# mLSTM heads in six PSUM banks, second attention with its value tile first, cosine products in PSUM, a reordered first stage, and attention weights brought to rows by transposing

## The chip, the cores and the metric

The kernel runs on one NeuronCore of a Trainium2 chip. A core has five engines with an instruction stream each: TensorE (PE), which multiplies matrices into PSUM, VectorE (DVE), ScalarE (ACT), GpSimd (POOL) and SyncE (SP), which here issues the DMAs of the weights. They meet through semaphores. SBUF holds operands; PSUM has 8 banks of 128 x 512 float32. The metric is the device time of one execution in microseconds.

## What is computed

Two blocks over 512 tokens of 1024 channels, one batch, float32. Cut to what matters:

```python
def first_block(x, ...):                   # mLSTM and pooling
    u = rms_norm(x, norm_in_g[l]); proj = u @ w_in[l]      # 4096 columns
    # pooling branch: window means (2, 4, 8, 16) minus u, a 256x256 map per group, scale, times silu(gate)
    # mLSTM branch: conv of 5 taps, silu, block-diagonal q, k, v, gates, 4 heads of 256
    h_fwd = mlstm_chunkwise(qh, kh, vh, log_i[0], log_f[0])
    h_bwd = flip(mlstm_chunkwise(flip(qh), flip(kh), flip(vh), ...))
    h = h_fwd + h_bwd                      # num / max(|den|, exp(-m)) in each direction
    h = (h - mu) * rsqrt(var + EPS)        # per token and head
    out = h * mh_norm_w + skip_w * c       # then times silu(gate)
    x = x + concat(pool, mlstm) @ w_out[l]
def second_block(x, ...):
    # i = 0: NSA attention (compressed, selected, window branch; 16 heads of 64, 4 key groups)
    # i = 1: sliding-window attention (SWA): 16 heads, 2 key groups, biases, a sink in the softmax denominator
    x = x + mixer(rms_norm(x, norm_mix[i]))
    x = x + (silu(causal_conv(a)) * u) @ w_down           # gated FFN of 2816 channels
    return rms_norm(x, norm_final)
def apply_rope(x, cos, sin): ...          # x*cos + swapped(x)*sin, on queries and keys
```

## The kernel before

**Tiles.** Activations lie channel-major, as 8 tiles of 128 channels x 512 tokens. Every projection is a list of weight tiles of 128 x 1024: `in` 32, `wo_pool` 8, `wo_m` 8, `nsa` 21, `nsa_o` 8, `gu0` 44, `down0` 22, `swa` 10, `swa_o` 8, `gu1` 44, `down1` 22, in all 227. SP loads them in turn into 4 buffers (`raw`); the load of tile w waits for `tile_split` of tile w-4. ACT rounds a tile to its high part (`high(w)`, the cast of L424), POOL subtracts that from it for the low part (L390, signal `tile_split`), both into 2 buffers. PE multiplies high by high, high by low and low by high for each of 8 channel tiles k: 24 matmuls of 128 x 512 (L1470 to L1472, `channel_major`) into one bank, signal `tile_used`. DVE or ACT takes the bank (`freed`). The activations are split the same way (`xh_ready`, `xl_ready`).

**Order.** Every engine's program is written out by hand; no scheduler is at work. `RING` and `BANK` say which PSUM bank a tile of a stage goes to.

**The start.** ACT casts weight tile 0, makes eight x_hi (L442), casts tile 1, squares the eight x tiles for the norm (`square`, L434; each from the fourth on waits for an addition of DVE, L817), issues the DMAs of 13 constants from its own queue (`constants`, L415), casts tile 2. DVE makes eight x_lo (L809). The 32 `in` tiles come in the order conv (8), pooling (8), pooling gate (8), mLSTM gate (8).

**From `in` to the heads.** PE merges k and v maps, computes k1 (banks 2 and 3 in turn, `k_out`), transposes values (`vt_mm`, DVE copies `vt_out`), and computes gates. DVE first makes the eight low parts for `wo_pool` (L837, line 952 is the copy of the values that PE waits for) and then the value copies.

**The heads.** For head h: `wo_pool` tiles of `POOL_TILES`, `maxima_rows(h+1)`, `head_scores(h+1)` into banks 2 to 5, then `numerators(h)`: for each of 4 token tiles i and 2 directions a sum of matmuls 128 x 257 (L1611) into bank n % 2:

```python
n = 8 * h + 2 * i + d
if n >= 2:
    pe.wait_ge((fwd_out, bwd_out)[d], NT * h + i)
```

So PE waits at each token tile until ACT (`forward_out`, L508) and DVE (`head_out`, L1020) have emptied the bank of the tile before. ACT's exponentials of the decay (L531) go into 2 buffers `WE`. After the last head ACT and DVE normalise H (`xhat`, `xhat_last` L1061), PE transposes it, DVE adds the skip term (`add_skip`, L1052), POOL multiplies by the gate (L396), and ACT copies each result as the high part of `wo_m`'s input (L554), for which `wo_m`'s first tile waits at L1447.

**NSA.** `rotary` (L1099 on, in `nsa` and in `swa`) is four DVE operations: sine product (L1104) and cosine product (L1105) into SBUF, a shuffle (L1111), a sum (L1115). In `nsa` the two products read PSUM. Attention goes through 48 units (token tile, heads in one or two pairs, branch): `score`, DVE's row maxima, ACT's exponentials, `turn` (PE transposes, L1743), ACT and DVE copies (L686), `output` (L1764). The softmax weights of a unit, one number per token and head, are spread over the channels by matmuls of an identity with a broadcast column (L1756).

**SWA.** `norm(4)` runs after tile 1 of the projection. Tile j: DVE multiplies by 1/rms into an SBUF buffer `TB` (L1392), ACT adds the bias there (`add_bias`, L768), DVE turns it (`rotary`, all operands in SBUF). Tile 0 is the key, 1 to 8 the queries, 9 the values, which PE transposes (L1514) once the last has its bias. Then come 16 units of two pairs.

## Time and profile before

| quantity | value |
|---|---|
| median of 3 runs | 1728.25 us (1727.33 to 1728.44) |
| the profiled execution's own time | 1723.56 us |
| its span in the trace | 1721.6 us |
| mean granted TensorE clock | 0.985 |
| PE busy | 1637.9 us, 95% |
| first SWA weight tile, first matmul | 1154.50 us |
| NSA attention units | 590 to 749.89 us |

The page gives the busy time of each engine; the trace gives every instruction with start, length, the idle time before it and what ended that. Matmuls of a row overlap, so lengths add up to more than the time between starts. A clock of 1.00 is 2.4 GHz, 0.5 is 1.2 GHz.

### The profile page before, as it was taken

To read this page: it belongs to the slowest core of one execution; us is meant where nothing else is said; L and a number is where in the kernel's file an instruction comes from. 1 tells how busy PE (TensorE), PEld (TensorE's weight loads), DVE (VectorE), ACT (ScalarE), POOL (GpSimd) and SP (SyncE) were. 2 spreads that over 40 slices of the span, in tenths; PEclk is the share of its full clock that TensorE was granted. 3 is DMA by queue.
4 is the path that set the end of the run, shared out by engine and by line. 5 is a ranking of instruction groups with operands and counts; after the bars stand their busy time and mean duration, and the time that the engine had idled before them with its cause. 6 is when DMAs were issued, how large, how long until landed. Compare 5 with 4: busy or idle time off the path is not lost.

```text
span 1721.6 us, 21467 instructions
## 1 busy us (share of the span) xinstructions
PE 1637.9 (95%) x8324; PEld 1280.4 (74%) x8324; DVE 1011.3 (59%) x1390; ACT 632.4 (37%) x1228; POOL 648.2 (38%) x421
## 2 busy tenths in 40 slices
PE   6999998979999999999999999999799999999996
PEld 4888655657788766678888888887567888888884
DVE  5995244575884466645655555448662755556444
ACT  4222333253562566634222222233462422223223
POOL 2444301134442133234444444434234444444442
PEclk9999999989999999999999999999899999999998
DMA  6222201005221100013322223222101322222221
GB/s 233 98 91 96 82 13 37 25 25 189 86 98 62 38 2 2 2 38 98 98 94 94 96 97 110 98 86 91 45 2 62 98 98 96 95 94 97 97 98 49
DMA packets 37670, 133.83 MB, mean 78 GB/s; under 512 B 4609, under 2 KB 5057, under 8 KB 37057
## 3 DMA queue, kind: packets, MB, share of 16 engines
q1 hardware_dynamic: 34992, 123.22, 21.4%
q10 hardware_dynamic: 2576, 9.24, 1.5%
q8 instruction: 66, 1.08, 0.3%
q14 instruction: 36, 0.29, 0.1%
HBM read 130.35 MB, written 2.10 MB: 77 GB/s over the span
## 4 chain that ended last, share of the span: by engine, by line
PE 84%; DVE 8%; ACT 3%; issue 3%; POOL 1%; ACTq 0%; DMA 0%; DVEq 0%; POOLq 0%
PE ps L1470 17%; PE ps L1471 17%; PE ps L1472 17%; PE ps L1806 4%; PE ps L1804 4%; PE ps L1805 4%; PE ps L1728 3%; PE ps L1743 3%; PE ps L1764 2%; PE ps L1523 2%; PE ps L1756 1%; DVE sb_arena L1115 1%; PE ps L1611 1%; DVE sb_x_lo L809 1%; ACT sb_arena L674 1%
## 5 line engine op out<-in xcount | busy, mean ns | idle before, releaser
L390 POOL TENSOR_TENSOR sb_w_lo<-sb_raw,sb_w_hi 128x1024 fp32r<-128x1024 f32 x227 | 556.1, 2450 | 858.1 <-ACT sb_w_hi L424 829.8
L1470 PE MATMUL ps<-sb_x_hi,sb_w_hi 128*128 128x512 f32 x1384 | 545.2, 394 | 23.4 <-ACT sb_x_hi L442 10.6
L1471 PE MATMUL ps<-sb_x_lo,sb_w_hi 128*128 128x512 f32 x1384 | 541.5, 391 | 0.0
L1472 PE MATMUL ps<-sb_x_hi,sb_w_lo 128*128 128x512 f32 x1384 | 541.3, 391 | 0.0
L424 ACT CAST sb_w_hi<-sb_raw 128x1024 fp32r<-128x1024 f32 x227 | 238.6, 1051 | 622.4 <-PE ps L1472 448.3
L1470 PEld LDWEIGHTS ps<-sb_x_hi,sb_w_hi 128*128 128x128 f32 x1384 | 261.5, 189 | 83.9 <-POOL sb_w_lo L390 17.1
L1472 PEld LDWEIGHTS ps<-sb_x_hi,sb_w_lo 128*128 128x128 f32 x1384 | 261.6, 189 | 55.3
L1471 PEld LDWEIGHTS ps<-sb_x_lo,sb_w_hi 128*128 128x128 f32 x1384 | 261.7, 189 | 54.2 <-issue 0.7
L1329 DVE TENSOR_TENSOR sb_x_lo<-sb_arena,sb_x_hi 128x512 fp32r<-128x512 f32 x44 | 98.4, 2243 | 104.4 <-ACT sb_x_hi L728 104.4
L1806 PE MATMUL ps<-sb_x_hi,sb_w_lo 128*128 128x512 f32 x336 | 130.7, 389 | 0.0
L1804 PE MATMUL ps<-sb_x_hi,sb_w_hi 128*128 128x512 f32 x336 | 130.7, 389 | 0.0
L1805 PE MATMUL ps<-sb_x_lo,sb_w_hi 128*128 128x512 f32 x336 | 130.7, 389 | 0.0
L1337 DVE TENSOR_TENSOR sb_arena<-ps,sb_rstd 128x512 f32<-128x512 f32 x44 | 30.4, 691 | 154.7 <-PE ps L1472 154.6
L1341 DVE SCALAR_TENSOR_TENSOR sb_arena<-sb_arena,sb_cols 128x512 f32<-128x512 f32 x44 | 115.8, 2632 | 1.6
L674 ACT ACTIVATE sb_arena<-ps,sb_small 128x256 f32<-128x256 f32 (+3 forms) x192 | 93.6, 497 | 55.9 <-DVE sb_small L1252 55.9
L723 ACT ACTIVATE sb_arena<-sb_arena 128x512 f32<-128x512 f32 x44 | 27.8, 633 | 150.5 <-DVE sb_arena L1343 150.4
L1252 DVE TENSOR_REDUCE sb_small<-ps 128x2 f32<-128x768 f32 (+3 forms) x48 | 50.3, 1048 | 53.0 <-PE ps L1732 53.0
L1728 PE MATMUL ps<-sb_arena 64*128 64x256 f32 (+3 forms) x384 | 74.5, 466 | 1.6 <-ACT sb_arena L781 0.9
L1806 PEld LDWEIGHTS ps<-sb_x_hi,sb_w_lo 128*128 128x128 f32 x336 | 63.1, 188 | 13.2
L1805 PEld LDWEIGHTS ps<-sb_x_lo,sb_w_hi 128*128 128x128 f32 x336 | 63.1, 188 | 13.2
L1804 PEld LDWEIGHTS ps<-sb_x_hi,sb_w_hi 128*128 128x128 f32 x336 | 63.1, 188 | 12.9
L1743 PE MATMUL ps<-sb_ident,sb_arena 128*128 128x128 f32 x432 | 59.7, 278 | 8.6 <-ACT sb_arena L686 6.3
(257 smaller groups left out, 1889.0 us busy)
## 6 DMA issues: line engine op xcount, KB each, us to landing
sb_raw<-in_w SPq DMA_DIRECT2D x227, 512.0 KB, 3.3
sb_resid<-in_x SPq DMA_DIRECT2D x8, 256.0 KB, 6.0
sb_arena<-in_cmp_w1k ACTq DMA_DIRECT2D x1, 2048.0 KB, 10.5
sb_arena<-in_cmp_w1v ACTq DMA_DIRECT2D x1, 2048.0 KB, 14.5
out<-sb_resid SPq DMA_DIRECT2D x8, 256.0 KB, 2.1
sb_arena<-in_pool_w ACTq DMA_DIRECT2D x1, 1024.0 KB, 5.0
sb_arena<-in_invc ACTq DMA_DIRECT2D x1, 1024.0 KB, 7.0
sb_arena<-in_wg ACTq DMA_DIRECT2D x1, 768.0 KB, 8.4
```

What stands on the lines that cost most here:

```text
L390: nc.gpsimd.tensor_tensor(WL[:, w % SPL], raw[:, w % RAW], WH[:, w % SPL].bitcast(F32), ALU.subtract).then_inc(tile_split, 1)
L424: nc.scalar.copy(WH[:, w % SPL], raw[:, w % RAW]).then_inc(hi_made, 1)
L674: ins = nc.scalar.activation(PE_[:, v % 2, hh, n * r:n * (r + 1)], PS[:, 2 + 2 * (v % 2) + hh, n * r:n * (r + 1)], ACT.Exp, bias=nmr[:, v ...
L1341: step.mark(nc.vector.scalar_tensor_tensor(CV[:, b], AP_[:, b, 1:1 + S], w[1], CV[:, b], ALU.mult, ALU.add))
L1470: mm(out, WH[:, s, k], XH[:, k], start=(k == 0), stop=False)
L1471: mm(out, WH[:, s, k], XL[:, k], start=False, stop=False)
L1472: ins = mm(out, WL[:, s, k], XH[:, k], start=False, stop=(k == KT - 1))
L1728: mm(s_[hh], QN[half, c + r, P * i:P * (i + 1)], K[half, k0:k0 + n], start=True, stop=False)
L1743: ins = nc.tensor.transpose(PS[:, 6 + hh, P * n:P * (n + 1)], PE_[:, v % 2, hh, P * n:P * (n + 1)], ident[:])
L1804: mm(psum(k), WH[:, s, k], XH[:, x], start=False, stop=False)
L1805: mm(psum(k), WH[:, s, k], XL[:, x], start=False, stop=False)
L1806: ins = mm(psum(k), WL[:, s, k], XH[:, x], start=False, stop=(f == FT - 1))
```

## The change

1. **Start.** DVE splits weight tile 0 in place of ACT and POOL; x tiles come from SP's and ACT's queues in turn; the first gain's columns are a DMA of their own; the 13 constants are issued by SP, behind the loads of weight tiles 0 to 3 and ahead of tile 4's. PE takes tile 0 in the order high x high, low x high, high x low (`first_tile`), tile 1 with its low part last. The `in` tiles are interleaved (`IN_ORDER`).
2. **After `in`.** Value copies and low parts alternate on DVE; a copy of k1 waits for its own tile of `xl_ready`, no longer for all eight; the first score tile goes ahead of the gate placement.
3. **Heads.** Numerators take banks 2*(i%3)+d; `WE` has 8 buffers; ACT and DVE interleave head h+1's decay with head h's output; both directions' denominators are one DVE operation; one `wo_pool` tile per head; the last one and the transposes of the finished heads lie around the last head's numerators; `wo_m`'s first high parts don't wait for the whole of `wo_pool`.
4. **Rotation.** The cosine product is written back into the PSUM bank that it reads.
5. **Both attentions.** DVE writes the weight of a unit spread over 64 channels (`WN`), and PE transposes that.
6. **SWA.** The value tile comes first; `norm(4)` after tile 2; scaling, bias and rotation happen in the tile's own PSUM bank; the last query tile lies between scores and the first turn; queries 8 and 9 are turned inside the attention; the projection starts when one `down0` tile is added, not eight; unit order changed.

```diff
+IN_ORDER = [t for n in range(8) for t in (2 * n, 2 * n + 1, 16 + n)] + list(range(24, 32))
+SWA_ORDER = [9, *range(9)]
-RING = {"in": [0, 1, 2, 3, 4, 5, 6], ..., "swa": [0, 1, 2, 3, 4, 5]}
+RING = {"in": [0, 1, 2, 3, 4, 5, 6], ..., "swa": [4, 5, 2, 3, 0, 1, 4, 6, 0, 1]}
...
+            dve.wait_ge(raw_in[0], 16)
+            nc.vector.tensor_copy(WH[:, 0], raw[:, 0]).then_inc(w0_hi, 1)
+            dve.wait_ge(w0_hi, 1)
+            nc.vector.tensor_tensor(WL[:, 0], raw[:, 0], WH[:, 0].bitcast(F32), ALU.subtract).then_inc(w0_lo, 1)
...
-            for k in range(KT):
-                lo("wo_pool", k, SZ[:, k])
-
             nc.vector.memset(V1[:, :, :, 256:257], 1.0)
             for j in range(KT):
                 dve.wait_ge(vt_mm, j + 1)
...
+                lo("wo_pool", j, SZ[:, j])
...
             def numerators(h):
                 pe.wait_ge(p_ready, 8 * (h + 1))
                 for i in range(NT):
+                    if i == NT - 1:
+                        pe.wait_ge(fwd_out, NT * h + 1)
+                        pe.wait_ge(bwd_out, NT * h + 1)
                     for d in range(2):
-                        n = 8 * h + 2 * i + d
-                        if n >= 2:
-                            pe.wait_ge((fwd_out, bwd_out)[d], NT * h + i)
...
-                            ins = mm(PS[:, n % 2, 0:257], PW[d][:, at:at + P], V1[:, j, h], ...)
+                            ins = mm(PS[:, 2 * (i % 3) + d, 0:257], PW[d][:, at:at + P], V1[:, j, h], ...)
...
+            for h in range(HEADS - 1):
+                maxima_rows(h + 1)
+                numerators(h)
+                head_scores(h + 1)
+                pe.wait_ge(fwd_out, NT * (h + 1))
+                pe.wait_ge(bwd_out, NT * (h + 1))
+                channel_major("wo_pool", 4 + h, KT)
...
+            turn_head(0)
+            turn_head(1)
+            numerators(HEADS - 1)
+            for j in range(2, 6):
+                turn_head(j)
...
+            channel_major("wo_pool", KT - 1, KT)
+            for j in range(6, KT):
+                turn_head(j)
             linear("wo_m")
...
-            def rotary(src, c_, s_, out, scale, signal, first=None):
...
+            def rotary(src, c_, s_, out, scale, done):
+
+                dve.wait_ge(freed, done - 1)
                 step.mark(nc.vector.scalar_tensor_tensor(TS, src, -scale, s_, ALU.mult, ALU.mult))
-                ins = nc.vector.scalar_tensor_tensor(TM, src, scale, c_, ALU.mult, ALU.mult)
...
+                step.mark(nc.vector.scalar_tensor_tensor(src, src, scale, c_, ALU.mult, ALU.mult))
                 step.mark(nc.vector.stream_shuffle(TS, TS, swap))
                 step.wait()
...
-                nc.vector.tensor_tensor(out, TM, TS, ALU.add).then_inc(rope_in, 1)
+                nc.vector.tensor_tensor(out, src, TS, ALU.add).then_inc(freed, 1)
...
-                        for hh in range(2):
-                            mm(PS[DH * hh:DH * hh + DH, v % 2, P * (2 + r):P * (3 + r)],
-                                     wn[:, v % 4, hh, r:r + 1].broadcast_to([P, DH]), ident[:], start=True, stop=True)
+                        nc.tensor.transpose(PS[:, v % 2, P * (2 + r):P * (3 + r)], WN[:, v % 2, r], ident[:])
...
-            pe.wait_ge(down_added, KT)
-            linear("swa", 10, 4)
-            turn_values(10, TB[:, 1], qb_ready, 10, 5)
-            pe.wait_ge(tok_out, 5)
-            pe.wait_ge(rope_in, 14 + 9)
-            attention(SWA_UNITS, len(NSA_UNITS), True)
+            pe.wait_ge(down_added, 1)
+            linear("swa", 9, 4)
+            attention(SWA_UNITS, len(NSA_UNITS), True, None, lambda: channel_major("swa", 9, 10))
```

The order of the instructions at three places. ACT at the start, from the cast of weight tile 1 on (`raw_in1` is its DMA, `sq_acc` DVE's additions), before:

```order
L424 CAST sb_w_hi<-sb_raw 128x1024 [waits raw_in1]
L434 ACTIVATE sb_arena<-sb_resid 128x512 x3
L434 ACTIVATE sb_arena<-sb_resid 128x512 [waits sq_acc] x5
L415 DMA sb_arena<-in_wqkv 128x96 [waits zero_set]
L415 DMA sb_arena<-in_bdm 128x32
L415 DMA sb_arena<-in_pool_w 128x2048
L415 DMA sb_arena<-in_invc 128x2048
```

and now:

```order
L452 CAST sb_w_hi<-sb_raw 128x1024 [waits raw_in1]
L462 ACTIVATE sb_arena<-sb_resid 128x512
L462 ACTIVATE sb_arena<-sb_resid 128x512 [waits sq_acc] x5
L452 CAST sb_w_hi<-sb_raw 128x1024 [waits tile_used,raw_in2]
L474 ACT_TABLE_LOAD
L474 ACTIVATE sb_small<-sb_small 128x1
L476 ACTIVATE sb_arena<-ps,sb_small 128x512 [waits sq_sum]
```

The cast of tile 2 stands directly behind the squares; 13 DMA instructions stood there. PE at the numerators of the first head (128x257), before, one bank per direction:

```order
L1611 MATMUL ps<-sb_arena 128x257 [waits p_ready,freed]
L1611 MATMUL ps<-sb_arena 128x257 x4
L1611 MATMUL ps<-sb_arena 128x257 [waits fwd_out]
L1611 MATMUL ps<-sb_arena 128x257
L1611 MATMUL ps<-sb_arena 128x257 [waits bwd_out]
L1611 MATMUL ps<-sb_arena 128x257 x2
```

and now (L1739 is the next head's maxima, L1670 its scores):

```order
L1739 MATMUL ps<-sb_arena,sb_ident 128x512
L1754 MATMUL ps<-sb_arena 128x257 [waits freed,p_ready]
L1754 MATMUL ps<-sb_arena 128x257 [waits freed]
L1754 MATMUL ps<-sb_arena 128x257 x13
L1754 MATMUL ps<-sb_arena 128x257 [waits bwd_out,fwd_out]
L1754 MATMUL ps<-sb_arena 128x257 x4
L1670 MATMUL ps<-sb_arena 128x512 [waits bwd_out,fwd_out]
```

Fifteen numerator matmuls stand ahead of the first wait for an emptied numerator bank. DVE in the SWA projection, before:

```order
L1392 TENSOR_TENSOR sb_arena<-ps,sb_rstd 128x512 [waits tile_used]
L1104 SCALAR_TENSOR_TENSOR sb_arena<-sb_arena 128x512 [waits rope_in,qb_ready]
L1105 SCALAR_TENSOR_TENSOR sb_arena<-sb_arena 128x512
L1111 STREAM_SHUFFLE sb_arena<-sb_arena 128x512 [waits dve_step]
L1115 TENSOR_TENSOR sb_arena<-sb_arena 128x512 [waits dve_step]
```

and now:

```order
L1488 TENSOR_TENSOR ps<-ps,sb_rstd 128x512 [waits tile_used] x2
L1194 SCALAR_TENSOR_TENSOR sb_arena<-ps,sb_arena 128x512 [waits freed,qb_ready]
L1196 SCALAR_TENSOR_TENSOR ps<-ps,sb_arena 128x512 [waits dve_step]
L1197 STREAM_SHUFFLE sb_arena<-sb_arena 128x512
L1199 TENSOR_TENSOR sb_arena<-ps,sb_arena 128x512 [waits dve_step]
```

All but the shuffle have an operand in PSUM now.

## Rows read from the trace of the kernel before

**Rows 1.** The page: the span, and part 1, busy time of each engine.

```profile
span 1721.6 us, 21467 instructions
...
PE 1637.9 (95%) x8324; PEld 1280.4 (74%) x8324; DVE 1011.3 (59%) x1390; ACT 632.4 (37%) x1228; POOL 648.2 (38%) x421
```

**Rows 2.** The windows view: us, busy PE, PEld, DVE, ACT, POOL, clock, DMA share, GB/s.

```profile
0.00:40.00 40.00, 23.73 (x76) 18.47 (x77) 22.68 (x27) 17.21 (x25) 10.47 (x11) 0.91 0.70 251
...
199.00:244.00 45.00, 40.80 (x163) 20.02 (x162) 18.78 (x29) 20.84 (x32) 2.37 (x1) 1.00 0.06 21
...
258.00:378.00 120.00, 103.95 (x399) 71.41 (x396) 63.10 (x202) 46.48 (x102) 17.12 (x9) 0.97 0.10 31
378.00:432.00 54.00, 48.98 (x196) 37.16 (x194) 33.83 (x35) 20.44 (x29) 29.18 (x14) 0.91 0.43 158
...
580.00:750.00 170.00, 164.07 (x1569) 109.92 (x1568) 107.91 (x247) 106.25 (x363) 50.87 (x111) 1.00 0.01 5
...
1154.00:1214.00 60.00, 56.16 (x241) 44.70 (x242) 52.85 (x61) 23.21 (x31) 24.12 (x10) 1.00 0.25 83
1214.00:1221.00 7.00, 0.53 (x3) 0.10 (x1) 6.71 (x9) 1.67 (x3) 2.50 (x2) 0.81 0.26 82
1221.00:1298.00 77.00, 68.84 (x596) 44.55 (x596) 44.85 (x117) 44.68 (x179) 21.07 (x59) 0.91 0.02 8
```

**Rows 3.** Who PE waited for, whole span: us in total, times, longest.

```profile
PE ps L1447 <- ACT sb_x_hi L554: 4.6, 7, 1.0
PE ps L1560 <- DVE sb_arena L952: 2.5, 1, 2.5
```

**Rows 4.** Timeline of the start: start, length, engine, line, operands, [idle before <-releaser].

```profile
10.65 0.77 PE L1470 MATMUL ps<-sb_x_hi,sb_w_hi 128*128 128x512 f32 x1 [10.65 <-ACT sb_x_hi L442]
...
27.67 1.04 ACT L424 CAST sb_w_hi<-sb_raw 128x1024 fp32r<-128x1024 f32 x1 [5.96 <-issue]
...
39.85 1.05 ACT L424 CAST sb_w_hi<-sb_raw 128x1024 fp32r<-128x1024 f32 x1 [8.11 <-PE ps L1472]
45.29 1.05 ACT L424 CAST sb_w_hi<-sb_raw 128x1024 fp32r<-128x1024 f32 x1 [4.38 <-PE ps L1472]
...
31.19 0.80 PE L1470 MATMUL ps<-sb_x_hi,sb_w_hi 128*128 128x512 f32 x1 [5.62 <-POOL sb_w_lo L390]
...
8.26 9.01 DVE L809 SCALAR_TENSOR_TENSOR sb_x_lo<-sb_resid,sb_cols,sb_x_hi 128x512 fp32r<-128x512 f32 x8 [8.26 <-ACT sb_x_hi L442]
17.18 5.46 DVE L817 TENSOR_TENSOR sb_arena<-sb_arena 128x512 f32<-128x512 f32 x7
```

**Rows 5.** PE in the heads: the group of the numerators, and one wait.

```profile
L1611 PE MATMUL ps<-sb_arena 128*128 128x257 f32 x160 | 40.2, 401 | 6.9 <-ACT sb_arena L508 5.0 <-DVE sb_arena L1020 1.1 <-DVE sb_resid L846 0.8
...
294.27 1.13 PE L1598 MATMUL ps<-sb_arena,sb_ident 32*128 32x512 f32 x4 [2.29 <-ACT sb_arena L531]
```

**Rows 6.** Timeline of POOL ahead of the second output projection.

```profile
377.75 11.39 POOL L396 TENSOR_TENSOR sb_arena<-sb_arena 128x512 f32<-128x512 f32 x7 [1.85 <-DVE sb_arena L1052]
```

**Rows 7.** PE in both attentions: the weight matmuls of the first, a piece of a unit of the second.

```profile
L1756 PE MATMUL ps<-sb_ident,sb_small 128*64 128x128 f32 x256 | 24.5, 291 | 0.3 <-DVE sb_arena L1295 0.3
...
1258.34 0.66 PE L1756 MATMUL ps<-sb_ident,sb_small 128*64 128x128 f32 x8
1258.83 1.03 PE L1764 MATMUL ps<-sb_arena 128*64 128x256 f32 x8
...
1261.95 1.06 PE L1743 MATMUL ps<-sb_ident,sb_arena 128*128 128x128 f32 x8 [0.17 <-ACT sb_arena L686]
```

**Rows 8.** DVE's rotation: one group of the first stage, then POOL and DVE in the second.

```profile
L1105 DVE SCALAR_TENSOR_TENSOR sb_arena<-ps,sb_arena 128x512 f32<-128x512 f32 x14 | 9.5, 681 | 0.0
...
1200.74 2.39 POOL L390 TENSOR_TENSOR sb_w_lo<-sb_raw,sb_w_hi 128x1024 fp32r<-128x1024 f32 x1 [3.12 <-ACT sb_w_hi L424]
...
1200.98 2.71 DVE L1115 TENSOR_TENSOR sb_arena<-sb_arena 128x512 f32<-128x512 f32 x1
```

**Rows 9.** PE at the end of the second attention's projection.

```profile
1221.77 1.12 PE L1514 MATMUL ps<-sb_ident,sb_arena 128*128 128x128 f32 x4 [7.24 <-ACT sb_arena L768]
```

583 lines of the change are left out of this document (355 added, 228 removed).

## The prediction

> **What bounds the kernel now.** I read the page first: TensorE is busy for 1637.9 of 1721.6 us [rows 1], and the weight tiles alone need 24 matmuls each on it. The change takes no weight tile away. So almost all that it can win is time in which PE stands still or runs at its low clock, and it can win that only in the stretches that it touches. The next view is the windows [rows 2], which I cut where PE's waits lie. PE's idle time is a stretch's length less its busy time, and (1 - clock) times the length is what the low clock costs in it, roughly, since only busy time counts:
>
> - 199 to 244: 45 - 40.80 = 4.2 us idle, clock 1.00.
> - 258 to 378, the heads: 120 - 103.95 = 16.1 idle, and 0.03 x 120 = 3.6 of clock.
> - 378 to 432, the second output projection: 54 - 48.98 = 5.0 idle, and 0.09 x 54 = 4.9 of clock.
> - 580 to 750, the NSA attention: 170 - 164.07 = 5.9 idle, clock 1.00.
> - 1154 to 1214, the SWA projection: 3.8 idle. 1214 to 1221: 6.5 idle, almost the whole stretch. 1221 to 1298, its attention: 8.2 idle, and 0.09 x 77 = 6.9 of clock.
>
> Then the waits and the timeline, to see what ends the idle time. For the value copies PE waits once for 2.5 us, and 4.6 us for the high parts of the second output projection [rows 3]. At the start PE stands 5.62 us ahead of 31.19; POOL, named as the releaser, had itself waited for the cast at 27.67, and that for 5.96 us of ACT's own DMA issues [rows 4].
>
> **The change part by part.** The sum is made against the profiled execution, 1723.56 us, which is 4.7 below the median of the runs; the forecast adds 4.7 again.
>
> *The start.* Of the 13 DMAs that ACT issued nothing is left on its queue; on SP's they stand behind tiles 0 to 3, so at worst tile 4 comes later, and its place is two tiles of PE work further on. Now the cast of tile 2 follows the squares, and these follow DVE's additions. The eight low parts took 9.01 us, one addition 5.46 / 7 = 0.78 [rows 4]. POOL's first split now waits for all eight, so I price these at 0.78 too: 6.2 us, from 8.26 to 14.5 (DVE's two new operations on weight tile 0 come before x is there). POOL's split of tile 1 then takes about 2.4, as at 1200.74 [rows 8], and holds one addition; six more end at 14.5 + 2.4 + 4.7 = 21.6, the last square a step before, at about 20.6. The cast (1.04) and the split (2.4) bring tile 2 to 24.1 in place of 31.19, 7.1 us. Tile 2 ran at half clock: ACT's casts, which wait for the ends of tiles, start at 39.85 and 45.29, so a tile takes 5.44, and tile 2 took 39.85 - 31.19 = 8.7. With no long stop ahead of it, 3.2 come back. Together 10.3, of which I take **10**. Bounds: 12 if tile 2 starts as soon as tile 1 ends, 6 if the squares end two or three us later. The new order of the `in` tiles I cost at nothing: PE is the cover, 5.44 us a tile, against conv work on DVE which now has two other tiles beside it. If the cover is gone a tile waits 1 or 2 us.
>
> *After `in`.* The copies of the values no longer stand behind eight low parts: 2.5 [rows 3], and the k1 copies, the exp tables and the early score tile take the rest of 4.2 [rows 2]. I take **4**, bounds 3 and 4.2.
>
> *The heads.* With two banks PE stopped at each token tile; the 160 numerator matmuls (40.2 us) had 6.9 us of idle time before them, and the exponentials in two buffers gave waits such as 2.29 us at 294.27 [rows 5]. With six banks fifteen matmuls go through, and what stands behind them (scores, a `wo_pool` tile of 5.44) covers ACT and DVE. What is recoverable is 16.1 + 5.0 + 3.6 + 4.9 = 29.6. What is late next is the tail behind the last head. Six of eight turned tiles can be skipped, gated and copied ahead; the last two can't. POOL's gate takes 11.39 / 7 = 1.63 each [rows 6], twice that is 3.3, an ACT copy and a DVE addition with their handovers some 1.2, and POOL's split of the next weight tile stands behind it, another 1.5 or so: 6 left. So **23.5**, bounds 15 (half of the idle time moves to other waits, with some clock) and 29.6. What could hold DVE here is told under the first rival.
>
> *Rotation.* In the first attention's projection the cosine product reads PSUM and takes 681 ns [rows 8]; written back to PSUM I price it the same. In SWA all operands were in SBUF, and there DVE's sum took 2.71 us at 1200.98 while POOL's split ran from 1200.74 to 1203.13 [rows 8]; the additions at the start, with POOL idle, took 0.78. DVE was busy for 52.85 of 60 us there [rows 2] and so set the pace. Now each operation but the shuffle has an operand in PSUM. Five operations of about 0.7 make 3.5 a tile against PE's 5.44: DVE catches up, even though `norm(4)` comes one tile later.
>
> *SWA.* Of the 3.8 idle in the projection I take 3. The stop of 7.24 us ahead of 1221.77 [rows 9] was the last tile's scaling, queued on DVE behind rotations, its bias on ACT and then the value transposes; with the value tile first that chain lies beside weight tiles, and the stop's 6.5 shrink to 0.5: 6. The low clock in 1214 to 1298 came with that stop; PE had been at 1.00 before it [rows 2]. Of its 6.9 I give back 5, since short waits remain. Of 8.2 idle in the attention I take 3.5, the turned weights in it. Sum **17.5**, bounds 13 and 22.
>
> *Weights by transposing.* In a unit of two pairs the eight weight records start at 1258.34 and the products with the values at 1258.83: 0.49. Eight transposes of the same size take 1.06 [rows 7], so two about 0.22: 0.27 less a unit of two pairs, and 0.16 less, in the same ratio, one of one pair. The first attention has 16 and 32 of them: 4.3 + 5.1 = 9.4 if PE were all that counts. It is not: units hang on maxima, exponentials and copies too, as the 0.17 for ACT before 1261.95 shows. DVE's wider write of the weights (128 x 128 or 256 in place of a few columns, some 0.2) lies in DVE's idle time, 170 - 107.91 = 62 us [rows 2]; uncovered it would cost up to 48 x 0.2 = 10 and leave no gain. I take **5**, bounds 0 and 8.5.
>
> Sum: 10 + 4 + 23.5 + 5 + 17.5 = 60. 1723.6 - 60 = 1663.6, and 4.7 more is **1668**.
>
> **The rivals.**
>
> *The heads give little (0.20).* DVE's normalisation and low parts there are SBUF operations, POOL's gate and splits run beside them, and DVE's sum shows what that does [rows 8]: 0.7 becomes 2.7. Eight such meetings cost 16 us of DVE time behind the last head. For it: PE's 4.6 us for the copies of ACT, which are downstream of POOL and DVE [rows 3]. Against: most of these operations now have a `wo_pool` tile and transposes in front of them. Gain 10 there in place of 23.5: 1682.
>
> *SWA stays bound by DVE (0.12).* If an operation that writes PSUM is held by POOL as one in SBUF is, or takes over a microsecond, a tile takes 5.5 again, and with the later norm the stop only moves. Gain 7 in place of 17.5: 1679. Against it: the mean of 681 ns over 14 operations [rows 8], in a stage in which POOL splits tiles as well.
>
> *Nearly all goes (0.15).* The upper bounds, 12 + 4.2 + 29.6 + 8 + 21 = 75: 1653. For it: each stop also brings a low clock, so what removes the one gives both.
>
> *Slower: the clock in the attentions (0.02).* Transposes take the place of matmuls in a stretch where they already are a large part. If PE's granted clock fell to 1.2 GHz there, each us of work would cost another. The work is 164.1 and, at full clock, some 62 us [rows 2], 226 in all; it decides when over 60 of that run at the low level, and with all of the first attention the time is 1668 + 164 = 1832. Against it: the clock is 1.00 over 580 to 750 with transposes in each unit [rows 2]. The Trainium skill has a rule that speaks for it, in "TensorE: Matmul & The Clock Gate", section "Part 4: PE-mode transpose": the full clock does not engage for transpose mode, which does not count as busy in the same way. By that rule more transposes could bring the low level; the trace shows none of it with the mixture that there is.
>
> **How the numbers follow.** The likeliest case has 0.48, with its own range 1658 to 1678. The first two rivals together (about 1692) have 0.015, and no gain by several partial failures 0.015, of which 0.01 lies within 0.2%. The range is 1650 to 1690: it holds the likeliest case, the first three rivals nearly whole, and leaves out both tails. About 0.2% (3.5 us) is what a measurement of this kernel can tell from no change. All cases but the last two lie far below that: faster 0.965, same 0.01, slower 0.025.
>
> **What the profile after would show.** Tile 2 starts at 23 to 25.5, and tile 3 at 29 to 31. Between 199 and 244 PE's busy share is over 97%. The numerators have under 2 us of idle time before them, and the first NSA tile comes 38 us or so earlier (10 + 4 + 23.5). DVE's last rotation operation in SWA takes 0.7 beside POOL's split. No stop over 2 us lies between the SWA projection and its attention, and the clock there is 0.97 or more. Units of the first attention are 0.1 shorter. The forecast is wrong if the waits reappear under other names: PE before `wo_m` waiting for ACT or POOL for more than 8 us, PE in SWA waiting for DVE at each tile, or PE in the attentions waiting for `weight` on DVE.

## The result, and the profile after

The changed kernel takes 1664.78 us (1663.86 to 1666.39) against 1727.85 (1727.33 to 1728.44): a ratio of 0.9636, 95% interval 0.9619 to 0.9653. It is 63.1 us faster. The forecast was 1668, range 1650 to 1690. The profiled execution took 1663.86 us, the sum had given 1663.6 for it. The 4.7 us that I added for the distance between the profiled execution and the median of before did not exist after: 0.9 us lie there now.

The page after, part 1, answers to [rows 1]:

```profile
span 1662.1 us, 20890 instructions
...
PE 1616.0 (97%) x8036; PEld 1267.8 (76%) x8036; DVE 994.2 (60%) x1360; ACT 630.1 (38%) x1230; POOL 645.7 (39%) x420
```

The span is 59.5 us shorter and PE busy for only 21.9 us less, so 37.6 us of the gain are idle time. The rest is PE at full clock for longer, with less to do, or with fewer restarts. The windows after (columns as in [rows 2]; PE's busy time is the second number, the clock the third from the right):

```profile
0.00:40.00 40.00, 32.34 (x116) 24.13 (x117) 28.06 (x31) 18.62 (x26) 12.79 (x12) 1.00 0.72 264
190.00:232.00 42.00, 41.00 (x165) 20.35 (x163) 19.05 (x29) 21.75 (x35) 2.37 (x1) 1.00 0.06 22
232.00:343.00 111.00, 110.85 (x467) 82.10 (x465) 64.09 (x168) 49.41 (x108) 24.50 (x13) 1.00 0.10 34
343.00:392.00 49.00, 44.59 (x183) 35.75 (x182) 29.70 (x33) 20.20 (x28) 23.16 (x11) 0.93 0.48 178
540.00:705.00 165.00, 156.83 (x1365) 101.79 (x1364) 115.66 (x246) 104.83 (x362) 50.90 (x111) 1.00 0.01 5
1108.00:1168.00 60.00, 59.68 (x274) 47.47 (x273) 47.47 (x73) 27.80 (x45) 24.80 (x10) 1.00 0.28 97
1168.00:1238.60 70.60, 62.09 (x475) 38.10 (x473) 50.89 (x131) 41.96 (x169) 23.34 (x60) 0.95 0.03 9
```

The 1.00 in the first row hides a low clock: the trace's records of the granted clock begin at 17 us. Before that the spacing of the matmuls shows it: 0.43 us apart up to about 17 us and 0.23 us behind, which are the levels of 1.2 and 2.4 GHz. The same holds for the 0.91 of before in [rows 2].

The heads (third row) have 0.15 us of idle time in 111, where [rows 2] had 16. The SWA projection (sixth) has 0.3, and the stop behind it is gone. What has not gone is in the fourth and the last row: 4.4 us idle and a clock of 0.93 in the second output projection, 8.5 idle and 0.95 in the SWA attention. Who PE waits for now:

```profile
PE ps L1911 <- ACT sb_arena L732: 11.0, 15, 2.2
PE ps L1595 <- ACT sb_x_hi L470: 7.7, 2, 7.5
PE ps L1560 <- ACT sb_x_hi L594: 4.4, 3, 3.0
PE ps L1583 <- DVE sb_arena L1382: 1.8, 2, 1.0
```

The first row is the turn of a unit's exponentials in both attentions, waiting for the copy out of the bank that it writes. The waits for numerators and for the value transposes of [rows 3], [rows 5] and [rows 9] are not in it.

Where the time went, from the first matmuls of weight tiles (and the last one of `in`) in both traces, beside my terms, all in us:

| from, to | before | after | gain | forecast |
|---|---|---|---|---|
| start, last matmul of `in` | 198.95 | 189.87 | 9.1 | 10 |
| to `wo_pool` tile 0 | 45.45 | 41.91 | 3.5 | 4 |
| to `nsa` tile 0 | 188.03 | 160.62 | 27.4 | 23.5 |
| to `nsa_o` tile 0 | 317.46 | 312.52 | 4.9 | 5 |
| to `swa` tile 0 | 404.61 | 403.63 | 1.0 | 0 |
| to `swa_o` tile 0 | 143.61 | 130.04 | 13.6 | 17.5 |
| to the end | 423.5 | 423.5 | 0.0 | 0 |

### The profile page after: what moved, and what is told of

Its sections match the earlier page's. It is cut to its first block, busy times and chain, and to the rows that moved or that the text cites. A ratio compares the mean times of both kernels' runs of the same rounds, so it can differ in the third digit from the quotient of the medians.

```text
span 1662.1 us, 20890 instructions
## 1 busy us (share of the span) xinstructions
PE 1616.0 (97%) x8036; PEld 1267.8 (76%) x8036; DVE 994.2 (60%) x1360; ACT 630.1 (38%) x1230; POOL 645.7 (39%) x420
## 4 chain that ended last, share of the span: by engine, by line
PE 89%; DVE 4%; issue 3%; ACT 2%; POOL 1%; DMA 0%; DVEq 0%; ACTq 0%; SPq 0%; POOLq 0%
PE ps L1583 18%; PE ps L1585 18%; PE ps L1584 18%; PE ps L1976 4%; PE ps L1977 4%; PE ps L1978 4%; PE ps L1896 3%; PE ps L1930 3%; PE ps L1911 3%; PE ps L1670 1%; ACT sb_arena L720 1%; PE ps L1754 1%; PE ps L1570 1%; PE ps L1640 1%; PE ps L1692 1%
## 5 line engine op out<-in xcount | busy, mean ns | idle before, releaser
L1583 PE MATMUL ps<-sb_x_hi,sb_w_hi 128*128 128x512 f32 x1368 | 536.9, 392 | 2.2 <-DVE sb_arena L1382 1.8
L1585 PE MATMUL ps<-sb_x_hi,sb_w_lo 128*128 128x512 f32 x1368 | 532.7, 389 | 0.0
L1584 PE MATMUL ps<-sb_x_lo,sb_w_hi 128*128 128x512 f32 x1368 | 532.5, 389 | 0.0
L1583 PEld LDWEIGHTS ps<-sb_x_hi,sb_w_hi 128*128 128x128 f32 x1368 | 257.1, 188 | 59.1 <-issue 3.0
L1584 PEld LDWEIGHTS ps<-sb_x_lo,sb_w_hi 128*128 128x128 f32 x1368 | 257.0, 188 | 54.3 <-issue 1.4
L1585 PEld LDWEIGHTS ps<-sb_x_hi,sb_w_lo 128*128 128x128 f32 x1368 | 256.9, 188 | 53.6
L1978 PE MATMUL ps<-sb_x_hi,sb_w_lo 128*128 128x512 f32 x336 | 130.7, 389 | 0.0
L1976 PE MATMUL ps<-sb_x_hi,sb_w_hi 128*128 128x512 f32 x336 | 130.7, 389 | 0.0
L1977 PE MATMUL ps<-sb_x_lo,sb_w_hi 128*128 128x512 f32 x336 | 130.7, 389 | 0.0
L1978 PEld LDWEIGHTS ps<-sb_x_hi,sb_w_lo 128*128 128x128 f32 x336 | 63.1, 188 | 13.1
L1976 PEld LDWEIGHTS ps<-sb_x_hi,sb_w_hi 128*128 128x128 f32 x336 | 63.1, 188 | 13.1
L1977 PEld LDWEIGHTS ps<-sb_x_lo,sb_w_hi 128*128 128x128 f32 x336 | 63.1, 188 | 13.0
```

The costliest lines, as they stand in the source:

```text
L1583: mm(out, WH[:, s, k], XH[:, k], start=(k == 0), stop=False)
L1584: mm(out, WH[:, s, k], XL[:, k], start=False, stop=False)
L1585: ins = mm(out, WL[:, s, k], XH[:, k], start=False, stop=(k == KT - 1))
L1976: mm(psum(k), WH[:, s, k], XH[:, x], start=False, stop=False)
L1977: mm(psum(k), WH[:, s, k], XL[:, x], start=False, stop=False)
L1978: ins = mm(psum(k), WL[:, s, k], XH[:, x], start=False, stop=(f == FT - 1))
```

## The experiments

Stage times below are those of this table, each from one profile. Two things limit what they tell.

A stop of 0.81 us ahead of `nsa` tile 0 is in some profiles (before, and runs 1, 2, 5, 8, 11 and 12) and not in others (after, and the rest). Behind it PE takes that tile at the pace at which ACT makes its high parts: pairs of matmuls start 0.54 to 0.62 us apart in place of 0.46, at a granted clock of 1.00. Together this is 2.2 us, 1.0 in the heads' stage and 1.2 in the next. What decides it was not tried. I call it the floating stop below; it makes spans less comparable than stages.

Stages that a run doesn't touch also differ. With the second attention as in the changed kernel its stage takes 129.1 to 130.7 us in eight profiles; the first attention with transposed weights takes 166.7 to 166.9 us, counted from the last `nsa` weight tile, in eleven. The medians of before that stand beside the runs lie between 1725.8 and 1728.7 us, so medians alone don't tell 2 us from nothing.

**1. The weights by matmul again.**

```diff
-                        nc.tensor.transpose(PS[:, v % 2, P * (2 + r):P * (3 + r)], WN[:, v % 2, r], ident[:])
+                        for hh in range(2):
+                            mm(PS[DH * hh:DH * hh + DH, v % 2, P * (2 + r):P * (3 + r)],
+                                     wn[:, v % 4, hh, r:r + 1].broadcast_to([P, DH]), ident[:], start=True, stop=True)
...
```

> The changed kernel with the softmax weights of both attentions spread by matmuls with a broadcast column again, nothing else undone. My account: the 4.9 us by which the first attention is shorter come from here, and part of the second one's too. 256 matmul pairs come back, 16 units x 0.27 and 32 x 0.16 on PE in the first (9.4), 16 x 0.27 in the second (4.3), of which about half shows: the first attention 4 to 6 us longer, the second 1 to 3, the kernel 1670 to 1673. Rival: the units are bound by the chain over maxima, exponentials and copies, and the attention got shorter by the other edits around it; then both stay within 1 us and the kernel at 1665 to 1666.

Measured: 1669.42 us, ratio 0.9658 (0.9643 to 0.9673). From the last `nsa` weight tile to `nsa_o` tile 0 it takes 170.33 us, as before (170.36), against 166.65 after: 3.7 us are the weights. The SWA stage is 0.4 longer (130.45), which lies within what that stage varies by. The rival for the first attention falls; for the second it holds.

**2. The weights alone, in the kernel before.**

```diff
-                        for hh in range(2):
-                            mm(PS[DH * hh:DH * hh + DH, v % 2, P * (2 + r):P * (3 + r)], ...)
+                        nc.tensor.transpose(PS[:, v % 2, P * (2 + r):P * (3 + r)], WN[:, v % 2, r], ident[:])
...
```

> The kernel before with only the softmax weights brought to rows by transposing. My account: it brings here what it brings in the changed kernel, 4 to 6 us in the first attention and 1 to 3 in the second: 1720 to 1723. Rival: in the second attention the clock is low for other reasons and the chain binds, so 4 to 5 in all. A low granted clock in the attentions from the transposes would show as a longer time, which I do not expect.

Measured: 1722.73 us, ratio 0.9976 (0.9965 to 0.9987). The first attention 166.72 against 170.36, so 3.6 us, the SWA stage 142.60 against 143.61, 1.0. The 4.6 in all are the rival's size; the 1.0 in the second attention is less than what its stage varies by. The windows view of the first attention, in the kernel before and in this run, each from its last `nsa` weight tile to its first of `nsa_o`:

```profile
579.53:749.89 170.36, 164.43 (x1571) 110.18 (x1569) 107.80 (x247) 106.25 (x363) 50.78 (x110) 1.00 0.01 5
...
584.31:751.03 166.72, 158.53 (x1378) 103.40 (x1377) 116.82 (x247) 106.26 (x363) 51.11 (x110) 1.00 0.02 5
```

PE is idle for 8.2 us where it was 5.9, and busy for 5.9 us less: that much the transposes took off PE, and 3.6 of it shows. DVE is busy for 9.0 us more, 0.19 for each of the 48 units, which is its wider write. The clock is 1.00 with 64 transposes more in it and 256 matmul records fewer (a float32 matmul leaves two records, a transpose one).

**3. Two banks for the numerators.**

```diff
-                    if i == NT - 1:
-                        pe.wait_ge(fwd_out, NT * h + 1)
-                        pe.wait_ge(bwd_out, NT * h + 1)
                     for d in range(2):
+                        if i >= 1:
+                            pe.wait_ge((fwd_out, bwd_out)[d], NT * h + i)
...
-                            ins = mm(PS[:, 2 * (i % 3) + d, 0:257], ...)
+                            ins = mm(PS[:, d, 0:257], ...)
```

> The changed kernel with the numerators in two banks again, one per direction, PE waiting at each token tile for the banks of the tile before; order and all else as changed. My account: the banks are the larger part of what the heads gained; the waits of before come back, 6.9 us over four heads, with some low clock: 8 to 14 us, 1673 to 1679, seen at the numerators. Rival: the order behind the numerators (scores, a weight tile) and the later statistics on DVE made the gain; then PE waits 1 to 3 us in all and the kernel is at 1666 to 1668.

Measured: 1682.28 us, ratio 0.9737 (0.9720 to 0.9754): 17.5 us slower than the changed kernel, more than either account. The wait, and for comparison the numerators of the changed kernel, which have none (the page's groups: busy, mean | idle ahead):

```profile
PE ps L1753 <- ACT sb_arena L539: 14.4, 12, 1.2
```

```profile
L1754 PE MATMUL ps<-sb_arena 128*128 128x257 f32 x160 | 35.7, 382 | 0.0
```

Twelve waits, three in each of the four heads, 1.15 to 1.23 us each, 14.4 in all; PE's numerators, stopped and restarted, are also busy for 38.9 us in place of 35.7, and with that the heads are 17.6 us longer (126.65 against 109.02). In the kernel before the waits had cost 6.9 us [rows 5].

Why so much more? One thing that changed in the order is that ACT makes the next head's exponentials between its outputs. That is not it: behind the last head ACT has none to make, and its three waits are as long. One of them, in this run:

```profile
336.90 2.40 PE L1753 MATMUL ps<-sb_arena 128*128 128x257 f32 x10
339.35 0.16 DVE L1092 SCALAR_TENSOR_TENSOR sb_dn<-ps,sb_arena 128x2 f32<-128x2 f32 x1 [1.27 <-PE ps L1753]
339.54 0.16 DVE L1094 TENSOR_TENSOR sb_dn<-ps,sb_dn 128x2 f32<-128x2 f32 x1
...
339.74 0.17 DVE L1096 RECIPROCAL sb_dn<-sb_dn 128x2 f32<-128x2 f32 x1
339.94 0.48 ACT L539 ACTIVATE sb_arena<-ps,sb_dn 128x256 f32<-128x256 f32 x1 [2.77 <-DVE sb_dn L1096]
340.46 2.44 PE L1753 MATMUL ps<-sb_arena 128*128 128x257 f32 x10 [1.15 <-ACT sb_arena L539]
```

The stop is a chain with nothing beside it: both directions' numerators end, DVE makes both denominators in three operations, ACT takes the forward bank out, and only then PE may write it again. Before, each direction had denominators of its own, so the forward bank was emptied while PE made the backward numerators, and the three waits of a head for ACT and DVE were 0.26 to 0.41 us in the first three heads (in the last, where ACT also normalised between its outputs, up to 2.29). So with two banks the joint denominators of the change cost more than the old ones; six banks hide them. No run had two banks with separate denominators in the new order, so this cause is read from the trace and not tried.

**4. Two buffers for the exponentials**, made behind the four outputs of a head, with DVE's products of a head in one piece.

```diff
-                    if n >= 8:
-                        act.wait_ge(p_ready, n - 7)
+                    if n >= 2:
+                        act.wait_ge(p_ready, n - 1)
...
                 for i in range(NT):
-                    decay(h + 1, i)
                     forward_out(h, i)
+                for i in range(NT):
+                    decay(h + 1, i)
```

> The changed kernel with two buffers for the decay exponentials in place of eight, and ACT making them behind the four outputs of a head, not between them (DVE's products of a head in one piece then). My account: waits of 1 to 2.3 us per head come back at the next head's scores or products, three or four times, 4 to 8 us: 1669 to 1673. Rival: a weight tile (5.44 us) and the scores stand in front of the next numerators and cover it: within 1 us of 1665.

Measured: 1665.50 us, ratio 0.9639 (0.9624 to 0.9653). `wo_pool` and heads take 109.86 against 109.02 us. The rival holds: scores and a weight tile cover the exponentials, and eight buffers bring under 1 us.

**5. The cosine product in SBUF**, for the second attention alone.

```diff
-                step.mark(nc.vector.scalar_tensor_tensor(src, src, scale, c_, ALU.mult, ALU.mult))
+                step.mark(nc.vector.scalar_tensor_tensor(cos, src, scale, c_, ALU.mult, ALU.mult))
...
-                nc.vector.tensor_tensor(out, src, TS, ALU.add).then_inc(freed, 1)
+                nc.vector.tensor_tensor(out, cos, TS, ALU.add).then_inc(freed, 1)
```

> The changed kernel with the cosine product of the second attention's rotation written to SBUF, so that the closing sum has all operands in SBUF; order, banks and all else as changed. My account: the sum is held while POOL splits a weight tile, 2.7 us in place of 0.7, DVE needs 5.5 us a tile against PE's 5.44 and can't catch up after the norm; the stop moves to the scores: 5 to 10 us longer, 1670 to 1675. Rival: the value tile's place is what counted, and DVE's length is covered by the banks: 0 to 2 us, 1665 to 1667, although the sum takes 2.7.

Measured: 1667.21 us, ratio 0.9648 (0.9634 to 0.9662); the SWA stage 131.88 against 130.04. The closing sum, in the kernel before, in the changed kernel, in this run, and in run 7 (groups by form of DVE: busy, mean ns):

```profile
L1115 DVE TENSOR_TENSOR sb_arena<-sb_arena 128x512 f32<-128x512 f32 x8 | 17.5, 2191 | 0.3
```

```profile
L1199 DVE TENSOR_TENSOR sb_arena<-ps,sb_arena 128x512 f32<-128x512 f32 x8 | 5.5, 692 | 0.3
```

```profile
L1200 DVE TENSOR_TENSOR sb_arena<-sb_arena 128x512 f32<-128x512 f32 x8 | 8.9, 1109 | 0.3
```

```profile
L1200 DVE TENSOR_TENSOR sb_arena<-sb_arena 128x512 f32<-128x512 f32 x9 | 14.2, 1581 | 0.3
```

My account falls in its size; the stage lies 1.2 us above the highest of the profiles with the product in PSUM, and the kernel just above the rival's range. The sum is held only sometimes, 1.1 us in the mean and not 2.7: with the other operations short, DVE waits for PE's tile. Four of the eight sums start 1.1 to 1.5 us behind the start of a split and take 1.4 to 1.8 us; the others take 0.69. In the kernel before, at 5.5 us a tile, six of eight started 0.22 to 0.25 us behind a split's start and took 2.7.

**6. The rotation alone, in the kernel before:** scaling, bias and cosine product in the tile's bank, old order of the tiles.

```diff
-                nc.vector.tensor_tensor(TB[:, j % 2], psum(b), rstd[:], ALU.mult).then_inc(freed, 1)
+                to = TB[:, 1] if j == 9 else psum(b)
+                nc.vector.tensor_tensor(to, psum(b), rstd[:], ALU.mult).then_inc(freed if j == 9 else q_scaled, 1)
...
+                    src = psum(BANK[t0 + j - 1])
...
+                    step.mark(nc.vector.scalar_tensor_tensor(src, src, scale, cs, ALU.mult, ALU.mult))
```

> The kernel before with the second attention's scaling, bias and rotation in the tile's own PSUM bank, the cosine product in place, tile order as before (key, queries, values last) and the norm after tile 1. My account: DVE's sum falls from 2.7 to 0.7 us beside POOL's split, DVE is at 3.5 us a tile, PE never waits in the projection, and the stop of 7.24 us before the value transposes shrinks to 3 to 4 (last scaling, bias, transposes, copy): 4 to 8 us shorter, 1720 to 1724. Rival: the stop is the chain behind the last tile whatever DVE's speed, and only the new order removes it: 0 to 2 us.

Measured: 1717.92 us, ratio 0.9959 (0.9945 to 0.9972). The SWA stage 137.98 against 143.61. PE at the value transposes, where it had stood 7.24 us [rows 9]:

```profile
1214.28 0.66 PE L1520 MATMUL ps<-sb_ident,sb_arena 128*128 128x128 f32 x4 [1.81 <-ACT sb_arena L768]
```

My account holds for the stop: most of it was DVE's backlog. The kernel is 9.5 us below the median of before, more than the 8 that I allowed. Of these 5.6 are in this stage and 2.3 in the two stages that the floating stop lengthens, which the profile of before has and this one has not.

**7. The order alone,** in the changed kernel, with every operand of the rotation in SBUF.

```diff
-                    nc.vector.tensor_tensor(psum(b), psum(b), rstd[:], ALU.mult).then_inc(q_scaled, 1)
+                    nc.vector.tensor_tensor(KC[:, j % 2], psum(b), rstd[:], ALU.mult).then_inc(q_scaled, 1)
...
-                rotary(psum(BANK[t0 + j]), cs, sn, ...)
+                rotary(KC[:, j % 2], cs, sn, ...)      # and the cosine product to TM
```

> The changed kernel with the second attention's scaling, bias and rotation all in SBUF (two buffers for the tiles, one for the cosine product); value tile first, norm, banks and the queries inside the attention as changed. Together with the kernel before with PSUM rotation alone (9.5 us shorter by the medians, 5.6 of them from the first SWA weight tile to the first one of its output projection) this is the other half. Revised account, after the run with only the cosine product in SBUF cost 1.8 us in this stage, not 5 to 10: the two edits remove the same stop, so either alone gets most of it. The stage took 143.6 before and 130.0 with the change; with the order alone 132 to 135, the kernel 1667 to 1670. Rival: the order needs a fast DVE, and with every operand in SBUF DVE is held at each tile again: the stage takes 138 or more.

Measured: 1670.73 us, ratio 0.9678 (0.9663 to 0.9692); the stage 135.18 us, just above the account's bound and below the rival's. Order alone 8.4, rotation alone 5.6, both 13.6: they add up within what the stage varies by, and don't stand for one another as I had thought after run 5.

**8. The constants on ACT's queue again.**

```diff
-            sp.wait_ge(zero_set, 3)
-            constants()
...
+            for dst, name in ((wqkv, "wqkv"), (bdm, "bdm"), (poolw, "pool_w"), ...):
+                act.dma_start(dst, a[name]).then_inc(consts_in, 16)
             high(2)
```

> The changed kernel with the 13 constant DMAs issued from ACT's queue again, between the squares and the cast of weight tile 2; SP issues none. My account: ACT's 6 to 6.6 us of issuing come back on the way to tile 2, which starts at 30 to 31.5 instead of 24.95 and runs at half clock in part: 6 to 9 us longer, 1671 to 1674. Rival: the start's gain came from splitting tile 0 on DVE and from x on two queues; then under 3 us come back, below 1668.

Measured: 1673.37 us, ratio 0.9699 (0.9682 to 0.9716). `in` ends at 199.40 in place of 189.87, and at 198.95 before: my account holds, and this one edit is worth the whole gain of the start. ACT, which issues for 6.19 us, and PE:

```profile
28.29 1.04 ACT L442 CAST sb_w_hi<-sb_raw 128x1024 fp32r<-128x1024 f32 x1 [6.19 <-issue]
...
31.80 0.80 PE L1578 MATMUL ps<-sb_x_hi,sb_w_hi 128*128 128x512 f32 x1 [6.55 <-POOL sb_w_lo L411]
32.39 0.63 PE L1579 MATMUL ps<-sb_x_lo,sb_w_hi 128*128 128x512 f32 x1
```

**9. ACT's first casts earlier.**

```diff
+            high(1)
+            for k in range(4):
+                square(0, k)
             act.wait_ge(cols_in, 16)
-            square(0, 0)
-            square(0, 1)
-            high(1)
-            for k in range(2, KT):
+            high(2)
+            for k in range(4, KT):
                 square(0, k)
-            high(2)
```

> The changed kernel with ACT's start in another order: the cast of weight tile 1 before the wait for the second part of the columns and the first squares, the cast of tile 2 after four squares. My account: tile 2 starts at 24.95 because PE's own work from 7.46 on, half of it at the low clock, ends there (the split of tile 2 ends at 24.9, in the same moment), so the new order brings under 0.5 us. Rival: the split was what bound it and tile 2 starts 1 us or more earlier.

Measured: 1665.75 us, ratio 0.9647 (0.9629 to 0.9666). Tile 2 starts at 25.73, not earlier than 24.95, though its split now ends at 22.2. PE works on tile 1 until 24.0, so the split alone was not the bound. Then the norm's sums, which stand ahead of tile 2, wait 1.2 us for DVE.

**10. Dummy matmuls ahead of the first tile,** with the casts early and the norm's sums behind tile 2.

```diff
+                pe.wait_ge(zero_set, 1)
+                for _ in range(36):
+                    nc.tensor.matmul(PS[:, 6, 0:P], ones[:], ones[:], start=True, stop=True)
                 pe.wait_ge(w0_hi, 1)
...
```

> The changed kernel with 36 dummy matmuls of 128 x 128 on PE from the first microsecond until its first operands are there, ACT's first casts ahead of most squares, and the norm's sums behind tile 2. In the changed kernel PE works from 7.46 to about 16.2 us at half clock; the dummies should bring it to full clock before. My account: some 4 us of PE time come back, tile 3 starts at 26 to 27.5 in place of 30.4: 3 to 4.5 us shorter, 1660 to 1662. Rivals: DVE's low parts (ready to 13 us) and POOL's splits bind as soon as PE is faster, then 1 to 2 us; or the clock does not follow the dummies, then under 1 us.

Measured: 1664.55 us, ratio 0.9644 (0.9630 to 0.9659). PE and DVE at the start (the timeline's columns, as in [rows 4]; the 36 dummies leave 72 records):

```profile
0.99 10.62 PE L1596 MATMUL ps<-sb_ones 128*128 128x128 f32 x72 [0.99 <-POOL sb_small L382]
11.36 2.10 PE L1600 MATMUL ps<-sb_x_hi,sb_w_hi 128*128 128x512 f32 x8
13.30 1.98 PE L1603 MATMUL ps<-sb_x_hi,sb_w_lo 128*128 128x512 f32 x8
...
28.28 0.79 PE L1585 MATMUL ps<-sb_x_hi,sb_w_hi 128*128 128x512 f32 x1
...
29.60 3.35 DVE L896 RECIPROCAL sb_rstd<-sb_arena 128x512 f32<-128x512 f32 x1 [5.37 <-ACT sb_arena L476]
```

The same in the changed kernel:

```profile
12.84 3.61 PE L1598 MATMUL ps<-sb_x_hi,sb_w_lo 128*128 128x512 f32 x8
...
24.95 0.50 PE L1583 MATMUL ps<-sb_x_hi,sb_w_hi 128*128 128x512 f32 x1
```

The clock does follow the dummies: the second eight matmuls take 1.98 us in place of 3.61. Tile 3 starts at 28.28, where my account had 26 to 27.5, and in the changed kernel at 30.51. PE starts its first tile 3.9 us later and is 2.2 us ahead at tile 3. But the reciprocal is 3.9 us later than the 25.71 of the changed kernel, PE waits 1.1 us for DVE at the first merged map, and 0.4 us are left at the end of `in`. The last of the rivals falls; what bound instead was the norm's chain, which none of them had named.

**11. The same, with the norm's sums inside tile 2.**

```diff
+                    if stage == "in" and j == 2 and k == 4:
+                        norm(0)
                     mm(out, WH[:, s, k], XH[:, k], start=(k == 0), stop=False)
```

> As the run with the dummy matmuls (33 now, not 36), but the norm's sums stand inside weight tile 2, behind its first four k, and not behind the tile. There tile 3 started 2.1 us earlier than in the changed kernel and only 0.4 us were left at the end of the projection, because DVE's reciprocal came 3.9 us later (29.60) and PE waited 1.1 us for DVE at the first merged map. My account: with the reciprocal at 26 to 27 the whole 2 to 3 us stay: first tile of the next projection at 228.5 to 230 in place of 231.8, the kernel 1661 to 1663. Rival: DVE is behind in this stage however early its norm comes, and gives back all but 0.5 us.

Measured: 1662.74 us (1661.84 to 1663.62), ratio 0.9622 (0.9609 to 0.9636). `in` ends at 187.82, 2.05 us earlier, and `wo_pool` tile 0 starts at 229.74, 2.04 earlier: the gain stays. The account holds. Its profile has the floating stop, so its span is only 0.3 us shorter. By the medians it is the fastest kernel here, but its interval overlaps that of the changed kernel: the trace shows the 2 us, and the timed runs don't settle it.

**12. The skip additions of tiles 6 and 7 ahead of the low parts.**

```diff
-            add_skip(4)
-            add_skip(5)
-            for k in range(4):
-                lo("wo_m", k, MZ[:, k])
-            for j in range(6, KT):
+            for j in range(4, KT):
                 add_skip(j)
-            for k in range(4, 6):
+            for k in range(6):
                 lo("wo_m", k, MZ[:, k])
```

> The changed kernel with DVE's skip additions of tiles 6 and 7 directly behind those of 4 and 5, ahead of the low parts of the second output projection. My account: PE waits 3.0 us at 347.6 (and 0.5 and 0.9 around it) for the high parts 6 and 7, which hang on these two additions, queued on DVE behind four low parts that run beside POOL's gating and take 1.05 each; PE takes all high parts before any low part, so the low parts can come later. 2 to 3.5 us shorter, 1661.5 to 1663. Rival: the low parts are then late, and PE waits for them as long: within 1 us of 1665.

Measured: 1665.63 us, ratio 0.9646 (0.9628 to 0.9664). The stop that was to go, in the changed kernel:

```profile
340.62 4.22 DVE L904 TENSOR_TENSOR sb_x_lo<-sb_arena,sb_x_hi 128x512 fp32r<-128x512 f32 x4
344.77 1.40 DVE L1115 SCALAR_TENSOR_TENSOR sb_arena<-ps,sb_cols,sb_arena 128x512 f32<-128x512 f32 x2
...
345.59 2.94 POOL L427 TENSOR_TENSOR sb_arena<-sb_arena 128x512 f32<-128x512 f32 x2 [2.49 <-DVE sb_arena L1115]
...
347.61 0.50 PE L1560 MATMUL ps<-sb_x_hi,sb_w_hi 128*128 128x512 f32 x1 [3.02 <-ACT sb_x_hi L594]
```

and PE's waits in the run:

```profile
PE ps L1560 <- DVE sb_x_lo L904: 1.9, 2, 1.2
PE ps L1556 <- ACT sb_x_hi L594: 1.9, 2, 1.0
```

The rival holds: 4.4 us of waiting became 3.8, half of it for the low parts. PE is through the high parts 2.9 us sooner (6.6 us in place of 9.5), but the eight low parts then take 5.65 us in place of 3.41, and the low clock, 6.8 us in both, begins 2.9 us later and lies over weight tiles: `wo_m` takes 52.6 us in place of 51.4. DVE has no idle time from 340.4 to 351 in this run and none from 340.8 to 348.1 in the changed kernel; it is the bound of this tail, and its order only says what is late.

## Why the prediction was right, by its steps

The numbers below are measured us of forecast us. The sum, 60 against 59.5 between the two profiles, is closer than its terms were: the heads came out 3.9 above their term and SWA 3.9 below, and that these cancel is luck. By the medians the gain is 63.1; the 3.6 us more are most of the 4.7 that I had added and that did not exist after.

**What bounds it.** Idle time of PE and its low clock in the touched stretches: this step carried. The stages that were not touched kept their length (423.5 to the end, before and after).

**The start.** 9.1 of 10. The path was the one named, ACT's issues on the way to tile 2 (run 8). Tile 2 starts at 24.95, forecast 24.1, and takes 5.6 us in place of 8.7, so the 3.2 us of low clock came back as priced. There my view of the bound was incomplete: POOL's split ends at 24.90, and PE itself is busy until then, because from 7.46 to about 17 it works at the low clock (runs 9 and 10). The split of tile 0 on DVE, the x tiles from two queues and the new order of the tiles bring nothing by themselves at the end of the stage: run 8 has them all and ends `in` at 199.40.

**After `in`.** 3.5 of 4. **The heads.** 27.4 of 23.5, of which 1.0 is the floating stop. The windows of exactly this stretch, before:

```profile
244.40:432.43 188.03, 165.66 (x650) 118.49 (x649) 104.51 (x247) 69.98 (x135) 49.61 (x23) 0.95 0.19 69
```

and after:

```profile
231.78:392.40 160.62, 156.06 (x651) 118.34 (x650) 94.41 (x200) 70.16 (x138) 47.66 (x23) 0.98 0.22 78
```

Idle time fell from 22.4 to 4.6, which is 17.8, and the cost of the clock from 0.05 x 188 = 9.4 to 0.02 x 160.6 = 3.2, which is 6.2; that leaves some 3 us. They lie in PE's own work: the numerators, busy for 40.2 us with their stops [rows 5], take 35.7 without them. The tail that I had priced at 6 is 4.4 of idle time and 3.4 of low clock, in the place named. Six banks are necessary for it with joint denominators (run 3); eight buffers are not (run 4).

**The weights.** 4.9 of 5, partly by luck: 3.7 are the weights, 1.2 the floating stop. The estimate was near (3.6 to 3.7 where I took 5), but PE's own saving was 5.9 and not 9.4. Part of that is a slip: a unit of one pair has half the records of one of two, so half of 0.27 is 0.135 and not 0.16, and the 9.4 should have been 8.6. DVE's wider write, for which the prediction shows no row, is the 0.19 us a unit of run 2, near the 0.2 that I took. The rival with the clock did not come: 1.00 over the attention. The Trainium skill, in "TensorE: Matmul & The Clock Gate", section "Part 4: PE-mode transpose", says that the full clock does not engage for transpose mode. This case's rows don't bear that out for transposes among matmuls: the clock stands at 1.00 with 64 more of them, and eight transposes took 1.06 us [rows 7] but 1.93 us at the low clock (at 1232.15, under SWA).

**SWA.** 13.6 of 17.5, and the step that failed is a term of the sum: "Of 8.2 idle in the attention I take 3.5, the turned weights in it." Idle time there is 8.5 now, not 4.7. The weights bring 0.4 to 1.0, no more than the stage varies by, and the prediction names no single wait that the other part of the 3.5 should have ended. PE's two longest stops in the attention of before are at the turns of the first and of the last of the 16 units:

```profile
1230.10 1.11 PE L1743 MATMUL ps<-sb_ident,sb_arena 128*128 128x128 f32 x4 [2.06 <-ACT sb_arena L674]
...
1292.78 1.06 PE L1743 MATMUL ps<-sb_ident,sb_arena 128*128 128x128 f32 x8 [1.74 <-ACT sb_arena L686]
```

After, there are two as long again, at the turns of the third and of the last unit:

```profile
1176.69 0.63 PE L1911 MATMUL ps<-sb_ident,sb_arena 128*128 128x128 f32 x4 [2.21 <-ACT sb_arena L732]
...
1232.15 1.93 PE L1911 MATMUL ps<-sb_ident,sb_arena 128*128 128x128 f32 x8 [2.10 <-ACT sb_arena L732]
```

Ahead of the first of these lie the queries that are turned inside the attention now:

```profile
1170.78 0.69 DVE L1194 SCALAR_TENSOR_TENSOR sb_arena<-ps,sb_arena 128x512 f32<-128x512 f32 x1 [0.73 <-ACT ps L827]
...
1172.88 0.69 DVE L1199 TENSOR_TENSOR sb_arena<-ps,sb_arena 128x512 f32<-128x512 f32 x1
1173.49 0.68 DVE L1339 TENSOR_REDUCE sb_small<-ps 128x4 f32<-128x512 f32 x1
...
1174.68 0.20 ACT L717 ACTIVATE sb_small<-sb_small 128x4 f32<-128x4 f32 x1 [3.70 <-DVE sb_small L1343]
```

The last query's rotation, which itself waits 0.73 us for ACT's bias, stands on DVE ahead of the next row maxima (L1339). ACT's exponentials wait 3.7 us, PE 2.2, and the clock is 0.80 from 1174 to 1180. It is 0.80 again from 1230 to 1238.6, behind the second stop, where it had been 1.00 in the last 8.6 us before. So the clock gave back 3.4 and not 5, and stands at 0.95 over the attention where the prediction's sign was 0.97 or more. That the turned queries cause the first stop is read from the trace; no run had them ahead of the attention. The terms for the projection (3.5 of 3) and the stop (6.5 of 6) held. DVE at 3.5 us a tile was right, but that PSUM operands are what frees it was only half of the matter: runs 5 and 7 show that how long a sum with both inputs in SBUF is held depends on where it falls against POOL's split.

**The rivals.** "The heads give little" was far off: normalisation and low parts do meet POOL (four low parts take 4.22 us), but there a weight tile and transposes lie in front of PE. "SWA stays bound by DVE" did not come.

## What to carry to other kernels

Read the gain of a rearrangement from idle time and low clock in the stretches that it touches, and take it nearly whole where one named wait ends the idle time, but at little or nothing where the idle time is many short waits of a chain over several engines. Parts of a change need not add up: the waits that extra banks were to remove were 6.9 us in the old code, and taking the banks away cost 17.5 once both directions shared their denominators, while order and faster rotation in SWA added up within half a microsecond. If an operation moves earlier to free one engine, look at what that engine's late result starts (here a reciprocal), or the gain is handed back one stage on.

## What the runs showed of the hardware

A DVE operation with two SBUF inputs took 0.69 us with POOL idle, and up to 2.7 beside POOL's 2.4 us split [rows 8]; with one input in PSUM it took 0.69 beside the split too. The Trainium skill, "SBUF — State Buffer", section "Who interferes with whom", says that a DVE instruction with two SBUF inputs contends with a GpSimd one that reads SBUF, over a pair of ports that is an exclusive lock. The trace agrees: the sum that started at 1200.98 ended at 1203.69, 0.56 us behind the split's end at 1203.13 [rows 8]. How often they meet is a matter of phase: the mean was 2191 ns before, 1581 in run 7, 1109 in run 5.

Matmuls on constants raised the clock of the first real tile: 1.98 us for eight matmuls against 3.61. Their records come every 0.21 us up to 5.8 us and every 0.11 from there on, and the records of the granted clock begin at 5.9 us in that trace, not at 17. In run 11 both happen at 4.2 us.
